# A hybrid encoder trunk on one core: out-projection weights in exchanged slots and other steps, GpSimd's low weight parts ahead of its clearing, the totals' inverse first in its step

## What is computed

```python
h = rms_norm(x, mix_pre_g[l])
(mq, mkv, mkr, gq, gk, gv, gg, gr, rq, rk, rv, rg) = jnp.split(h @ w_in, offsets, axis=-1)
# eight softmax heads (MLA): q and k,v from low-rank latents, chunk-causal mask
# four gated linear heads (GLA), four retention heads: rms_norm(o) * silu(gate)
m = jnp.concatenate([o_mla, o_gla, o_ret], axis=-1) @ w_out
x = x + rms_norm(m, mix_post_g[l])
```

## Time and profile before

| | us |
|---|---|
| median of 3 runs | 1922.75 (1921.42 to 1924.51) |
| the profiled execution, its own time | 1917.17 |
| its span, first to last instruction | 1915.4 |
| TensorE busy in it | 1879.2 (98%) |
| VectorE, ScalarE, GpSimd busy | 1238.2, 815.1, 656.4 |
| waits of TensorE with a named releaser, all below 5 us in total each | 28.5 together |
| mean granted clock of TensorE | 0.994 of full speed |

### The profile page before, as it was taken

How to read it: one execution, slowest core, us unless ns; L and a number is a source line. 1 busy time by engine, 2 the same in 40 slices (tenths; PEclk the granted TensorE clock), 3 DMA queues, 4 the chain that set the end, 5 groups by cost and what they waited for, 6 DMA issues and landing times.

```text
span 1915.4 us, 31029 instructions
## 1 busy us (share of the span) xinstructions
PE 1879.2 (98%) x12664; PEld 1689.3 (88%) x12664; DVE 1238.2 (65%) x1620; ACT 815.1 (43%) x1182; POOL 656.4 (34%) x500
## 2 busy tenths in 40 slices
PE   8999999999989999999999999999999899999998
PEld 7999988887668999998899999889867699999886
DVE  6888843534655888862578888344465568888533
ACT  5344433325564444442343444233356544444321
POOL 3666500002331566620046664001033326666000
PEclk9999999999999999999999999999999999999999
DMA  4223233231012132233312332332200311322321
GB/s 156 89 110 109 100 120 132 89 118 44 2 58 97 67 110 93 104 129 113 132 45 89 109 110 110 132 132 96 87 24 2 111 67 67 110 103 100 127 99 67
DMA packets 27227, 179.96 MB, mean 94 GB/s; under 512 B 3283, under 2 KB 3445, under 8 KB 7158
## 3 DMA queue, kind: packets, MB, share of 16 engines
q1 hardware_dynamic: 25618, 173.63, 25.1%
q10 hardware_dynamic: 1508, 4.94, 0.8%
HBM read 176.45 MB, written 2.10 MB: 93 GB/s over the span
## 4 chain that ended last, share of the span: by engine, by line
PE 93%; DVE 3%; issue 1%; ACT 1%; POOL 1%; DMA 0%; SPq 0%; POOLq 0%; ACTq 0%; DVEq 0%
PE ps L510 28%; PE ps L512 28%; PE ps L511 27%; PE ps L885 2%; PE ps L522 1%; PE ps L904 1%; PE ps L689 1%; PE ps L691 1%; PE ps L690 1%; PE ps L892 1%; PE ps L805 1%; PE ps L825 0%; PE ps L831 0%; DMA raw<-stream 0%; PE ps L546 0%
## 5 line engine op out<-in xcount | busy, mean ns | idle before, releaser
L510 PE MATMUL ps<-xH,WH 128*128 128x256 f32 (+2 forms) x1408 | 421.2, 299 | 0.4 <-DVE WL L1531 0.2
L512 PE MATMUL ps<-xH,WL 128*128 128x256 f32 (+2 forms) x1408 | 418.7, 297 | 0.0
L511 PE MATMUL ps<-xL,WH 128*128 128x256 f32 (+2 forms) x1408 | 418.7, 297 | 0.0
L510 PE MATMUL ps<-TH,WH 128*128 128x256 f32 x1216 | 344.1, 283 | 0.0
L511 PE MATMUL ps<-TL,WH 128*128 128x256 f32 x1216 | 344.1, 283 | 0.0
L512 PE MATMUL ps<-TH,WL 128*128 128x256 f32 x1216 | 344.1, 283 | 0.0
L1409 DVE TENSOR_TENSOR WL<-raw,WH 128x2048 fp32r<-128x2048 f32 x62 | 143.8, 2319 | 267.0 <-ACT WH L1010 254.0
L510 PEld LDWEIGHTS ps<-xH,WH 128*128 128x128 f32 (+1 forms) x1408 | 268.9, 191 | 9.2 <-issue 1.7
L511 PEld LDWEIGHTS ps<-xL,WH 128*128 128x128 f32 (+1 forms) x1408 | 268.8, 191 | 8.4 <-issue 1.0
L512 PEld LDWEIGHTS ps<-xH,WL 128*128 128x128 f32 (+1 forms) x1408 | 268.8, 191 | 7.6
L510 PEld LDWEIGHTS ps<-TH,WH 128*128 128x128 f32 x1216 | 233.5, 192 | 0.0
(11 more groups left out here) (302 smaller groups left out, 3703.3 us busy)
## 6 DMA issues: line engine op xcount, KB each, us to landing
raw<-stream SPq DMA_DIRECT2D x156, 1024.0 KB, 4.8
norm_g<-norm_gains SPq DMA_DIRECT2D x11, 512.0 KB, 4.5
x<-x_in SPq DMA_DIRECT2D x4, 512.0 KB, 7.0
wq<-w_q_up ACTq DMA_DIRECT2D x4, 512.0 KB
out<-x SPq DMA_DIRECT2D x4, 512.0 KB, 2.7
const<-consts ACTq DMA_DIRECT2D x2, 610.5 KB
wkv<-w_kv_up ACTq DMA_DIRECT2D x2, 512.0 KB
cos<-positions ACTq DMA_DIRECT2D x2, 256.0 KB
```

The lines of the kernel that those rows point to most:

```text
L510: mm(dst, wh, xh, start=start, stop=False)
L511: mm(dst, wh, xl, start=False, stop=False)
L512: return mm(dst, wl, xh, start=False, stop=stop)
```

## The change

It gives pair 8 slot 1 and pair 9 slot 0, and moves their halves: ScalarE's high halves of pair 8 from steps 21 and 22 to steps 3 and 6, of pair 9 from steps 24 and 25 to 27 and 28; VectorE's low halves of pair 8 from steps 23 and 24 to 7 and 10, of pair 9 from 28 and 29 to 29 and 30. The wait for the last `make_q` moves from pair 8 to pair 9. GpSimd makes `wkvL` ahead of its wait for pair 7 and of clearing `qx`. `spread_shares` follows `scores` or the output tile in its step on TensorE. `invert_totals` comes ahead of everything but `scale_heads` in its step on VectorE. The number of operations is the same.

```diff
@@ def slot_of(stage, i)
-        return {10: 4, 11: 5}.get(i, i % 2)
+        return {IN_PAIRS: 1, IN_PAIRS + 1: 0, 10: 4, 11: 5}.get(i, i % 2)
@@ TensorE, steps
-                        if n % 8 == 7:
-                            spread_shares(i - 1)
                         if n + AHEAD < STEPS:
                             scores(n + AHEAD)
                         else:
...
-                            down_tile(0, MIX_START[n + AHEAD - STEPS], mixed(0), True, False)
+                            down_tile(1, MIX_START[n + AHEAD - STEPS], mixed(0), True, False)
+                        if n % 8 == 7:
+                            spread_shares(i - 1)
...
-                        last = down_tile(0, d, mixed(0), True, False)
+                        last = down_tile(1, d, mixed(0), True, False)
...
-                    last_pairs(stage, base + IN_PAIRS + 1, (1, 4, 5), (mixed(1), mixed(2), mixed(3)))
+                    last_pairs(stage, base + IN_PAIRS + 1, (0, 4, 5), (mixed(1), mixed(2), mixed(3)))
@@ ScalarE
                 def high_half(base, i, j):
 
                     act.wait_ge(landed[(base + i) % 2], 16 * ((base + i) // 2 + 1))
-                    act.wait_ge(pair_done, base + i - 1)
+                    if i == IN_PAIRS:
+                        act.wait_ge(pair_done, base + IN_PAIRS)
+                    else:
+                        act.wait_ge(q_psum, due(q_psum, HEADS))
                     half = slice(j * SLAB, (j + 1) * SLAB)
-                    last = af(WH[:, i % 2, half], raw[:, (base + i) % 2, half], ACT.Copy)
+                    last = af(WH[:, (i + 1) % 2, half], raw[:, (base + i) % 2, half], ACT.Copy)
...
-                        if n in (21, 22):
-
-                            act.wait_ge(q_psum, due(q_psum, HEADS))
-                            high_half(base, IN_PAIRS, n - 21)
-                        if n in (24, 25):
-                            high_half(base, IN_PAIRS + 1, n - 24)
+                        if n in (3, 6):
+                            high_half(base, IN_PAIRS, n // 6)
+                        if n in (27, 28):
+                            high_half(base, IN_PAIRS + 1, n - 27)
@@ VectorE
-                    last = tt(WL[:, i % 2, half], raw[:, (base + i) % 2, half], WH[:, i % 2, half].bitcast(F32),
+                    last = tt(WL[:, (i + 1) % 2, half], raw[:, (base + i) % 2, half], WH[:, (i + 1) % 2, half].bitcast(F32),
                               ALU.subtract)
...
-                        if n in (23, 24):
-                            low_half(base, IN_PAIRS, n - 23)
+                        if n in (7, 10):
+                            low_half(base, IN_PAIRS, n // 10)
...
-                        if n in (28, 29):
-                            low_half(base, IN_PAIRS + 1, n - 28)
+                        if n in (29, 30):
+                            low_half(base, IN_PAIRS + 1, n - 29)
...
                             scale_heads(i - 2)
+                        if n % 8 == 6:
+                            invert_totals(i - 1)
                         ready = n < LIN_STEP or n < NORM_STEP and (n - LIN_STEP) % PARTS == 1
...
-                        if n % 8 == 6:
-                            invert_totals(i - 1)
                         if n + AHEAD < STEPS:
                             tops(n + AHEAD)
@@ GpSimd
                 nc.gpsimd.memset(attn_r[:].rearrange("p h i -> p (h i)"), 0.0)
+                pool.wait_ge(mix_landed, due(mix_landed, 16 * 7))
+                for j, high in ((1, wvH), (0, wkH)):
+                    half = slice(j * SEQ, (j + 1) * SEQ)
+                    pool.wait_ge(wkvH_ready, due(wkvH_ready, 2 - j))
+                    nc.gpsimd.tensor_tensor(wkvL[:, half], wkv[:, half], high[:].bitcast(F32),
+                                            ALU.subtract).then_inc(wkvL_ready, 1)
+                pool.wait_ge(wkvL_ready, due(wkvL_ready, 2))
                 pool.wait_ge(pair_done, base + IN_PAIRS)
                 pool.sem_inc(pool_passed)
                 nc.gpsimd.memset(qx[:].rearrange("p a b h i -> p (a b h i)"), 0.0).then_inc(cleared, 1)
...
-                pool.wait_ge(mix_landed, due(mix_landed, 16 * 7))
-                for j, high in ((1, wvH), (0, wkH)):
...
-                pool.wait_ge(wkvL_ready, due(wkvL_ready, 2))
                 pool.wait_ge(exp_ready, due(exp_ready, 3))
```

## The result

| | before | after |
|---|---|---|
| median, us | 1922.09 (four runs, 1917.87 to 1924.51) | 1902.18 (four runs, 1900.58 to 1903.00) |
| profiled execution, us | 1917.17 | 1901.88 |
| its span, us | 1915.4 | 1900.1 |
| mean granted clock | 0.994 | 0.997 |

The ratio is 0.9898, with a 95% interval of 0.9879 to 0.9917: faster by 1.0%. Timed again beside eleven runs of before it was 0.9903 (0.9888 to 0.9917), 1900.27 against 1919.19. The prediction had 1907.2 and a gain of 15.6 us, with 1903.0 as the fast end: the direction was right, the gain was larger than the sum, and the time lies 0.8 us under the range. The profiled executions differ by 15.3 us, the medians by 19.9 and 18.9. The profiled execution of before (1917.17 us) is one of its faster ones; that of the changed kernel lies 0.3 us under its median.

A forecast was written before the change was run, and what follows sets the result against it. TensorE is busy nearly throughout, so only waits and low-clock time in each mixer's front and tail can be won: 5.9 + 6.1 + 3.6 = 15.6 us, 1917.2 to 1901.6 profiled, 1907.2 off the median; range 1903.0 to 1915.0.

The forecast's parts named there:

- Front, 2.3 us a layer: Ahead of each mixer's steps: making `wkvL` before the clearing removes TensorE's 2.3 us wait; with 1.3 for clock, 5.9 in all.
- the half which I took: Front: GpSimd's two early subtractions, about 2.8 us, may hold VectorE up by 0 to 2.8; 1.4 us was taken.
- The price in full: Rival, the lock in full: VectorE held up the whole 2.8 us in the front, sum 1.4 us smaller, 1908.6; chance 0.12.
- Middle, 0: Between front and tail TensorE waits for nothing, so pair 8's halves moved into early steps there cost nothing.
- Tail, the chain: Steps 21 to 28: VectorE relieved, `tops(27)` 3.3 us earlier, ScalarE then the bound; tail gains 6.1 us at the upper clock.
- I count one tail of each kind: Of the two layers' tails, one stays at the upper clock (6.1 us gained), one falls to the lower (3.6).
- The front's clock: Layer 0's front took 8.60 us against 7.30 in layer 1; the 1.3 us, put to the lower clock, goes with the wait.
- 1.7 us for the replay: Range's fast end: 1.7 us taken off the forecast's fast end for a replay that is too cautious, giving 1903.0.
- the two terms: Range's slow end: the front's clock (1.3 us) and lock (1.4 us) terms gone, on top of the first rival's 1911.7.
- Only the front: Rival: the tail is bound by something untouched, its waits only change names; 5.9 us gained, 1916.9, or 3.2, 1919.6; chance 0.10.
- a wait for a wait: Rival: ScalarE's dense steps, another VectorE stretch and low clock leave each tail 2.5 us; 11 in all, 1911.7; chance 0.16.
- slower: Rival: the `kf` wait in step 23 lowers the clock to the tail's end; 7 us slower, 1929.9; chance 0.04.

The follow-up runs named there:

- the front alone: Only GpSimd's `wkvL` subtractions moved ahead of its clearing, against the kernel before: 1911.74 us, ratio 0.9963.
- all but the front: The changed kernel with GpSimd's `wkvL` subtractions where they were before: 1909.57 us, ratio 0.9956 against the kernel before.
- The swaps alone: Only `spread_shares` put behind the scores and `invert_totals` first in its step, against the kernel before: 1923.98 us against 1917.90, ratio 1.0029.

## Why the prediction was right and wrong

**Front, 2.3 us a layer: right.** With both clocks up it is 7.30 - 4.72 = 2.6, 0.3 more than the wait. The held-up VectorE was 1.4 us in the sum: two operations were stretched by 1.12 and 0.25 us, and `ckvL` ended 1.4 us later against pair 7's end. That the half which I took was met so closely is luck in part; the two reasons given for it are both in the trace. The rule of the Trainium skill (SBUF — State Buffer, section "SBUF: two separate sides") describes how, and the trace agrees: the first operation ended 0.55 us after GpSimd's first subtraction, nearly its own length of 0.69. The price in full, 2.8 us, did not come about. One of the operations read PSUM and took its usual 0.69 us, and it seems that VectorE held GpSimd up in its turn (the first subtraction took 1.77 us, before 1.42).

**Middle, 0: nearly.** From line 935 to line 841 it is 53.35 us instead of 53.12, in both layers. The kernels with `invert_totals` early all have it (53.30 to 53.36), those without don't (53.10 to 53.16). The likely reason, not tested further, is that VectorE's totals now come ahead of `keep_low` in step 6.

**Tail, the chain: right.** `tops(27)` ended 10.47 us after `turn(21)` instead of 13.86, so 3.4 us earlier (3.3 predicted); `keep_turn(29)` ended 17.6 us after it (18.1 predicted); the waits are 0.7 to 1.0 for `kf` (1.1) and 0.87 for `keep_turn(26)` (1.1). The wait of 0.8 for `keep_turn(29)` did not come. The tail is 6.5 us shorter (6.1 predicted). That VectorE's amount of work was the bound is shown by the kernel with the low halves back. Behind it, `values(14)` to `values(15)` took 5.68 us, as before.

**The step that failed: "I count one tail of each kind".** I took the lower clock as a coin that the remaining waits leave as it was, and so put 2.5 us of the tails aside. It is not a coin. In the profiles of the kernel before (three) and of the front alone (one) all eight tails hold a stretch at the lower clock and take 29.10 us on average. In the profiles of the changed kernel, of its two copies without the front and of its repetition all eight tails run at the upper clock, 22.80 us on average. Each tail gained 6.3 us, both 12.6, not 9.7. Over all seventeen profiles the line is as sharp: with the low halves of pair 8 in steps 23 and 24 (six profiles) all 12 tails hold a low stretch, with them in steps 7 and 10 (eleven) none of 22 does.

The front's clock was mis-sized too, in the same direction: I priced it by one profile (1.3 us in one layer of two). Over the six fronts in the three profiles of before the mean is 8.25 us; over all twenty fronts without the wait it is 4.71 or 4.72. That is 3.5 us a layer, both 7.1, not 5.9. With the eight fronts of other kernels that keep the wait the mean is 8.66.

| us | predicted | mean over the profiles |
|---|---|---|
| front, both layers | 5.9 | 7.1 |
| tail, both layers | 9.7 | 12.6 |
| middle | 0 | -0.5 |
| low stretch after line 841 (2 of 8 places against 0 of 8, 1.6 us each, two places a run) | 0 | -0.8 |
| low stretch after lines 704 and 705 (4 of 8 against 2 of 8, 1.5 us each) | 0 | -0.8 |
| sum | 15.6 | 17.6 |
| spans, mean of three profiles of before less mean of two of the changed kernel (1916.7, 1899.2) | | 17.5 |
| medians, two comparisons | | 19.9 and 18.9 |

The sum agrees with the profiled executions. The 1.3 to 2.3 us by which the medians gained more must lie in executions without a profile, for the most part in those of before, the slowest of which took 1924.51 us; where they spent it is not shown.

The number missed by a second step as well. I carried the 5.6 us by which the median of before lay above its profiled execution over to the changed kernel: 1901.6 became 1907.2. There the median lay 0.3 us above (1902.18 against 1901.88). The ten timed executions of the changed kernel lie within 3.0 us of each other (1899.97 to 1903.00), the 34 of before within 8.1. So most of those 5.6 us belonged to the kernel before and went with the change, presumably with its low stretches.

That the two profiled executions differ by 15.3, nearly the prediction, is chance: the one after had two low stretches that cost 1.5 and 1.6 us, the one before was in the faster part of its kernel's range. The range was drawn on the tails both at the upper clock (1904.7) and 1.7 us for the replay; it had nothing for a front whose clock cost more than in the one profile. Its slow end is added up wrongly by a little: 1911.7 and the two terms make 1914.4, not 1915.0.

**The rivals.** "Only the front", "a wait for a wait" and "slower" are refuted by the tails. The rule's full price was not paid. The price of "slower" was also too high: it counts 15.8 us of work in the 19.0 us behind 1494, where TensorE was busy for 13.6 us, part of it at the lower clock. The parts don't add in time: 6.2 (front alone) and 8.3 (all but the front) make 14.5 of 18.9 to 19.9. The traces show why in part: with the wait left in, the fronts of the kernel without the front's change cost 9.84 and 10.07 us in one profile, 8.58 and 8.73 in another. None of the six fronts of the kernels that have the halves moved and the wait left in is the cheap one of 7.3 us, which three of the eight others are; why stays open.

## What to carry to other kernels

Where one engine is saturated in a short stretch (13.49 us busy of 13.90) while it idles twenty steps earlier, move work there that has no need to be late: with 2.8 us of subtractions put back the tails were 6.3 and 4.9 us longer, the clock's part included. Order inside a step is worth little beside it, and alone it made the kernel slower. A wait of a busy TensorE costs its length plus what the clock does next, and that part must be averaged over several profiles; one is not enough to price it.

## What the runs showed that was not expected

A wait of 2.32 us that is the same to 0.01 us in all seven profiles that have it cost 0, 1.3 to 1.6 or 2.5 to 2.8 us more at the lower clock, in the same place of the program (fronts of 7.3, 8.6 to 8.9, and 9.8 to 10.1 us).

The clock also fell where TensorE never waited: at 1466.4 us of the changed kernel, behind sixteen products of two columns each (line 841), for 3.4 us at a busy share of 1.00, and at 1353.7, behind products with 16 and 1 contraction rows (lines 704 and 705). That these products are the cause is not shown: the same ones stand in the other layer and in the other profiles without a fall. The fall behind line 841 came only with `spread_shares` behind the scores (10 of 20 against 0 of 14). A busy row in the profile does not say that the clock stays up.

The swaps alone made the kernel 0.29% slower although the sum of TensorE's waits in the tail was no larger: 10.7 us for `kb`, `ks_ret`, `kf`, `probT` and `prob` against 11.6 before (`ks_ret`, `krgg`, `probT`, `prob` and `kf`). Its profile has the clock low for longer in the tail of layer 1, and once more in that layer's step 15.
